# Expert up pass: two of three fetched token blocks summed on VectorE instead of one

## The reference

```python
idx = i1 * PEER_KEYS + i2                  # 8 heads x 16 picks = 128 expert rows for a token
g = jax.nn.softmax(cv, axis=-1)
u = expert_down[idx]
act = jax.nn.gelu(jnp.einsum('thkd,td->thk', u, xb).astype(jnp.float32), approximate=False)
v = expert_up[idx]
return jnp.einsum('thk,thkd->td', (g * act).astype(xb.dtype), v)
```

## Time and profile before

| | us |
|---|---|
| median of 3 runs | 4072.21 (4071.66 to 4079.16) |
| profiled execution | 4068.46 |
| its span, first to last instruction | 4066.7 |
| TensorE busy | 3796.6 (93%) |
| VectorE busy | 2708.6 (67%) |
| GpSimd busy | 1820.8 (45%) |
| ScalarE busy | 1664.8 (41%) |

### The profile page before, as it was taken

The page is one execution under the profiler, slowest core; times in us unless marked ns, Lnnn a source line. Parts: engine busy times, 40 slices in busy tenths (PEclk is TensorE's granted clock), DMA queues, the critical chain, the costliest instruction groups (busy, mean ns, idle before and its releaser), DMA issues. The chain is left out here.

```text
span 4066.7 us, 57361 instructions
## 1 busy us (share of the span) xinstructions
PE 3796.6 (93%) x21102; PEld 3193.4 (79%) x21102; DVE 2708.6 (67%) x4934; ACT 1664.8 (41%) x3225; POOL 1820.8 (45%) x1291
## 2 busy tenths in 40 slices
PE   6999899989899969998999999999969999999998
PEld 3877688866677869998999999999956777777776
DVE  3587411148775426688999999997756666666666
ACT  2111233358422431136777777777612222222222
POOL 3333233359544112133333333335546767676774
PEclk8999899999999989999999999999989999999999
DMA  4244333348666332276888888889999999999998
GB/s 158 69 150 150 120 97 124 103 160 263 183 196 190 103 123 73 62 259 231 269 274 274 266 281 268 271 272 352 364 309 349 352 347 350 336 336 349 347 349 290
DMA packets 641664, 957.80 MB, mean 236 GB/s; under 512 B 198900, under 2 KB 418820, under 8 KB 640516
## 3 DMA queue, kind: packets, MB, share of 16 engines
q1 hardware_dynamic: 311984, 407.35, 30.5%
q0 software_dynamic: 110592, 402.70, 28.3%
q10 hardware_dynamic: 218836, 144.47, 11.3%
HBM read 807.46 MB, written 146.93 MB: 235 GB/s over the span
## 5 line engine op out<-in xcount | busy, mean ns | idle before, releaser
L2034 POOL DMA_INDIRECT down_rows<-in_peer_down_dram,row_ids x384 | 464.3, 1209 | 830.3 <-DVE row_u L2174 743.4
L2055 PE MATMUL p_u<-h2T_hi,downT_hi 128*128 128x320 f32 x2048 | 657.2, 321 | 11.3 <-ACT gelu_out L2105 10.6
L2055 PE MATMUL p_u<-h2T_lo,downT_hi 128*128 128x320 f32 x2048 | 637.6, 311 | 0.0
L2055 PE MATMUL p_u<-h2T_hi,downT_lo 128*128 128x320 f32 x2048 | 637.3, 311 | 0.0
L2174 DVE CUSTOM_DVE_ANT_0 gate_rows<-down_rows,x_tok_rows 128x1024 f32<-128x1024 f32 x384 | 469.1, 1222 | 79.8 <-DMA down_rows<-in_peer_down_dram,row_ids 66.7
L2576 PE MATMUL p_y<-up_hi,coef_hi 128*128 128x512 f32 x1240 | 493.3, 398 | 18.6 <-DVE coef_lo L2468 9.2
L2576 PE MATMUL p_y<-up_lo,coef_hi 128*128 128x512 f32 x1240 | 485.9, 392 | 0.0
L2576 PE MATMUL p_y<-up_hi,coef_lo 128*128 128x512 f32 x1240 | 483.9, 390 | 0.0
L545 PE MATMUL p<-hT_hi,w_hi 128*128 128x512 f32 x1024 | 410.4, 401 | 7.1 <-POOL w_lo L499 7.1
L2055 PEld LDWEIGHTS p_u<-h2T_hi,downT_hi 128*128 128x128 f32 x2048 | 390.2, 191 | 13.7 <-issue 12.7
L545 PE MATMUL p<-hT_hi,w_lo 128*128 128x512 f32 x1024 | 399.9, 391 | 0.0
(11 more groups left out here) (337 smaller groups left out, 8081.1 us busy)
## 6 DMA issues: line engine op xcount, KB each, us to landing
down_raw<-in_peer_down_dram SPq DMA_DIRECT2D x128, 512.0 KB, 5.6
up_raw<-in_peer_up_dram SPq DMA_DIRECT2D x128, 512.0 KB, 5.7
scratch_gu<-gelu_out ACTq DMA_DIRECT2D x128, 320.0 KB, 5.1
gelu_in<-scratch_gu SPq DMA_DIRECT2D x128, 320.0 KB, 6.1
weights_in<-scratch_w SPq DMA_DIRECT2D x128, 320.0 KB, 6.9
w_raw<-in_w_in_dram SPq DMA_DIRECT2D x64, 512.0 KB, 4.2
scratch_w<-weights_out ACTq DMA_DIRECT2D x40, 512.0 KB, 8.1
scratch_w<-y_acc ACTq DMA_DIRECT2D x40, 512.0 KB, 7.0
```

Source lines behind the costliest of these rows:

```text
L2034: pool.indirect_dma_start(out=rows[:, c % RING, :], out_offset=None, in_=inp["peer_down"][0], in_offset=bass.IndirectOffsetOnAxis(ap=row_i ...
L2055: mm = pe.matmul(ps_u[half][:, 0:HD], d[:, n % 3, k, :], h2[h][:, k, half * HD:(half + 1) * HD], start=(j == 0), stop=(j == 3 * KD - 1))
```

## The change

Two of the three fetched blocks are now summed on VectorE (`NP = 1`, `NO = 2`): own fetches and own sums run over blocks 1 and 2, two a tile step, with a ring of 4; block 0 alone goes through TensorE, one quad a group, at slot 1, with a ring of 4. The first spread is made before the first group and each further one a group ahead. On GpSimd the four row fetches of a group stand behind the first low part and its own fetches (in group 1 behind the third). The id copy for the own blocks takes two blocks at a time. At the end, blocks 1 and 2 are finished first.

```diff
-    NP = NA - 1
-    OWN = NA - 1
-    FINISH = (*range(NP - 1), OWN, *range(NA, TB - 2), NP - 1, TB - 2, TB - 1)
-    RING = 6
+    NP = NA - 2
+    NO = NA - NP
+    FINISH = (*range(NP - 1), *range(NP, NA), *range(NA, TB - 2), NP - 1, TB - 2, TB - 1)
+    RING = 4
     SPREADS = 2 * NP
-    RING_OWN = 2
+    RING_OWN = 4
...
                 def fetch_own(c):
 
+                    a, k = NP + c // P, c % P
...
-                                            in_offset=bass.IndirectOffsetOnAxis(ap=ids_t[:, OWN, c:c + 1], axis=0)
+                                            in_offset=bass.IndirectOffsetOnAxis(ap=ids_t[:, a, k:k + 1], axis=0)
...
                 cut(0, 0)
                 cut(0, 1)
-                for r in range(4):
+                for r in range(RING):
                     fetch(r)
                 fetch_own(0)
+                fetch_own(1)
                 cut(0, 2)
                 cut(0, 3)
-                for r in range(4, RING):
-                    fetch(r)
-                fetch_own(1)
+                fetch_own(2)
+                fetch_own(3)
                 for g in range(1, GROUPS):
-                    r, c = (g - 1) * 4 * NP + RING, (g - 1) * GT + RING_OWN
-                    cut(g, 0)
-                    fetch_own(c)
-                    for i in range(4):
-                        fetch(r + i)
-                    cut(g, 1)
-                    fetch_own(c + 1)
-                    cut(g, 2)
-                    fetch_own(c + 2)
-                    for i in range(4, 8):
-                        fetch(r + i)
-                    cut(g, 3)
-                    fetch_own(c + 3)
-                for r in range((GROUPS - 1) * 4 * NP + RING, 4 * QUADS * NP):
-                    fetch(r)
-                for c in range((GROUPS - 1) * GT + RING_OWN, P):
+                    c = (g - 1) * GT * NO + RING_OWN
+                    for j in range(GT):
+                        cut(g, j)
+                        for i in range(NO):
+                            fetch_own(c + j * NO + i)
+                        if j == (2 if g == 1 else 0):
+                            for i in range(4):
+                                fetch(4 * g + i)
+                for c in range((GROUPS - 1) * GT * NO + RING_OWN, P * NO):
                     fetch_own(c)
...
                 def add_own(c):
...
-                    dve.wait_ge(own_added, c)
-                    dve.scalar_tensor_tensor(acc[:, OWN, :], own_rows[:, c % RING_OWN, :], coef[:, OWN, c:c + 1],
-                                             acc[:, OWN, :], ALU.mult, ALU.add).then_inc(own_added, 1)
+                    dve.scalar_tensor_tensor(acc[:, a, :], own_rows[:, c % RING_OWN, :], coef[:, a, k:k + 1],
+                                             acc[:, a, :], ALU.mult, ALU.add).then_inc(own_added, 1)
...
+                for q in range(NP):
+                    spread_rows(q)
                 for g in range(GROUPS):
                     for j in range(GT):
                         coefs(g, j)
                         if g:
-                            add_own((g - 1) * GT + j)
+                            for i in range(NO):
+                                add_own(((g - 1) * GT + j) * NO + i)
...
-                    for q in range(NP):
-                        spread_rows(g * NP + q)
+                    if g + 1 < GROUPS:
+                        for q in range(NP):
+                            spread_rows((g + 1) * NP + q)
...
                 done = 0
-                for j in range(GT):
-                    add_own((GROUPS - 1) * GT + j)
+                for i in range(GT * NO):
+                    add_own((GROUPS - 1) * GT * NO + i)
...
                             if base == 0:
                                 pe.wait_ge(g_lo_done, j + 1)
                                 pe.wait_ge(up_lo_done, j + 1)
-                            elif j % 2:
-                                quad(j // 2)
+                            elif j == 1:
+                                quad(0)
```

More of the change, by code:

```diff
@@ L2414, in _ @@
                         act.wait_ge(rows_kept, t + 1)
-                    elif t == OWN:
-                        act.wait_ge(own_added, P)
+                    elif t < NA:
+                        act.wait_ge(own_added, P * (t - NP + 1))
                     else:
@@ L2452, in add_own @@
                     dve.wait_ge(own_loaded[c % RING_OWN], 16 * (c // RING_OWN + 1))
[L2453 to L2454 removed]
+                    a, k = NP + c // P, c % P
+                    if c:
+                        dve.wait_ge(own_added, c)
+                    if k == 0:
+                        dve.tensor_scalar(acc[:, a, :], own_rows[:, c % RING_OWN, :], coef[:, a, 0:1], None, ALU.mult
                                           ).then_inc(own_added, 1)
                         return
[L2457 to L2459 removed]
+                    dve.scalar_tensor_tensor(acc[:, a, :], own_rows[:, c % RING_OWN, :], coef[:, a, k:k + 1],
+                                             acc[:, a, :], ALU.mult, ALU.add).then_inc(own_added, 1)
                 def coefs(g, j):
```

4 lines of the change are left out of this document (1 added, 3 removed).

## The result

The changed kernel takes 4198.05 us (median of 4 runs, 4187.55 to 4202.84), the kernel before, run beside it, 4072.1 (4071.66 to 4079.16). The ratio is 1.03, with a 95% interval of 1.0281 to 1.032. The prediction was 4089 us with a range of 4034 to 4110: the sign was right, the size far off. The profiled execution took 4202.84 us (span 4201.0), 134.4 us more than the one of before.

What follows compares the result with a forecast made beforehand. TensorE bounds the kernel before; after the change a VectorE-GpSimd loop would. Steady part +17, start -5, end +5 make +17 us on the profiled 4068.46, 4085.5; that run lay 3.7 under the median, so 4089 us, range 4034 to 4110.

Steps and rivals of the forecast that it cites:

- a loop of VectorE and GpSimd: Steady groups: 25.7 us of work plus 6.8 of collisions, 32.4 us against 31.85, +17 us over 30 groups; chance 45%.
- 25.7 us a group: VectorE's own work in a group of four steps and one spread, without collisions; alone it would fit under TensorE's 29.59.
- product at 17.3, just ahead of the low part (17.4): Step 3 of a group: product goes first, low part runs 18.1 to 20.4, coefficient low part is delayed, 1.5 us lost.
- 1.2, 1.5 and 1.7 to 1.9: Microseconds lost a group to GpSimd's low parts: before step 2's product, in step 3, and in next group's step 0.
- the fourth, the own sum: Step 2: GpSimd's low part gets in between the pair's two own sums at 12.6, runs until 15.0; 2.4 us lost.
- The claim of stability: Group loop: moving GpSimd half a microsecond either way gives the same 32.3 to 32.4 us, trusted to about 0.5 us.
- 1.24: Microseconds after the end of a pair of own sums at which GpSimd's next low part asks, with two fetches a step.
- Late weights: Step 3's weights land at 17.2 against 17.3 wanted: no cost in the sum, but no cover behind it.
- loads late on top of the loop: Rival: step 3's weights land late and lengthen every group; at +1 us, +47 us, 4119 us; chance 12%.
- Start: Before group 1: GpSimd skips the first quad's wait, loads come earlier; gain of 5 us, at most 11, at least -4.
- End: After the last step: eight own sums instead of four, two rounds of fetching in a ring of four; +5 us.
- The bound by DMA: Rival: DMA full at 362 GB/s, 30.4 us a group (30.6 with idle), 4034 us; DMA or TensorE bound, chance 28%.

Runs made afterwards that it cites:

- low_on_dve: Changed kernel with the tiles' low parts moved from GpSimd to VectorE, right behind each coefficient low part: 4033.03 us, ratio 0.9912.
- memset_low: Changed kernel with each GpSimd low part replaced by three memsets of the same tile, reading nothing from SBUF: 4051.65 us.
- low_first: Changed kernel with GpSimd reordered: low part directly behind a pair of own sums, ahead of the fetches, row fetches two a step in two steps: 4065.37 us, ratio 0.9989.
- gap_wait: Changed kernel with a one-column GpSimd memset between fetch and low part, the low part waiting for its semaphore: 4137.48 us.
- wait_both: Changed kernel with the first own fetch of a step waiting for both own sums in place of one: 4203.0 us.
- no_weights: Changed kernel loading the expert weights of only the first two tiles and using them for all: 4163.0 us.
- short_low: Changed kernel with GpSimd's low part over 64 of 1024 columns, the others left zero: 4066.72 us.
- order_only: Kernel before, with only the changed kernel's order of row fetches in group 1 and of spreads: 4073.14 us, ratio 0.9995.
- low_between: Changed kernel with low parts on VectorE, between gelu product and coefficient low part, where VectorE waited for ScalarE: 3990.76 us, ratio 0.9797.

## Why the prediction was wrong

**Right.** TensorE stops being the bound, and a loop of VectorE and GpSimd sets the pace. low_on_dve and memset_low show that the collision of the low parts with two-input operations is the cause, low_first that the order on GpSimd decides its size. The work on VectorE was well priced: 25.7 us a group, and 25.7 + 9.2 (lines above, per group: products 4 x 1.05, own sums 8 x 0.24, spread 2.64, `coef_lo` 4 x 0.1) + 0.9 late weights is 35.8 of the 35.98. That one pair in four carries a low part inside it was right too.

**The step that failed: "product at 17.3, just ahead of the low part (17.4)".** The prediction let the one that asks first in the record go first. The earlier trace rows have it so for a low part that GpSimd had waited for (0.66 us idle). All four low parts of a group stand directly behind a fetch here, with their inputs ready, and there a lead of up to 0.62 us is no lead. Instead of going first, or of losing 1.2 to 1.9 us to a low part already under way, spread and products lose the whole low part, 2.6 to 2.7 us. Three such terms were priced 1.2, 1.5 and 1.7 to 1.9 and came out at 2.63, 2.71 and 2.65; the fourth, the own sum, was priced 2.4 and is 1.95. gap_wait shows it by taking the head start away: blocked time falls to about 4.4 us a group (4 x 0.345 of products, 4 x 0.72 of `coef_lo`, 8 x 0.02 of own sums).

**A second error, of timing, beside it.** For the terms of 1.2 and of 1.7 to 1.9 the prediction had the low part start ahead of VectorE's operation, by 1.2 and 0.5 us. In the group shown the product is recorded 0.36 us and the spread 0.39 us ahead of it, because the fetches before it were held under VectorE's operations: counted from the pair that ended at 3839.35, the product stands at 7.85 us, as predicted (7.8), the low part at 8.2 and not at 6.6. By the prediction's own rule VectorE would have gone first in all three.

**The claim of stability failed with it.** "Moving GpSimd by half a microsecond either way ... gives the same 32.3 to 32.4" was said of a model in which the order of asking decides. The low part comes 2.10 us after a pair (3831.88 against 3829.78), not 1.24, because a fetch asked under the second sum is held. wait_both moved two of the low parts to 2.5 us and the time stayed, so half a microsecond does leave the sum as it is, but at 36 us and not at 32.3 to 32.4. No run puts the low part at 1.24 us, so what the timing alone is worth stays open; what the winner is worth gap_wait shows: 1.7 us a group with late weights that have grown from 0.8 to 3.6.

**Late weights: priced at nothing, with 0.1 us of cover.** In the changed kernel they add 0.9 us of waits a group; no_weights is 1.2 us a group shorter. Where the collisions shrink they take over: 3.6 us in gap_wait, 5.3 in short_low. The rival "loads late on top of the loop" was true in kind, and held back because the collisions were slower still. So 32.4 us was not reached in gap_wait either, where VectorE goes first: it takes 34.2.

**Start:** predicted -5, it was -2.0 in this profile and -1.8 in order_only. The prediction took only 5 of 11 us because of the transfers; the runs speak against that limit: with the same loads low_between takes 58.8 us there and memset_low 57.9, against 63.7. **End:** predicted +5, it was -2.6. Eight own sums stand there, but three follow at once (4155.99), and the fetch of the last lands in 5.32 us:

```profile
4155.99 1.20 DVE y_acc L2454
4157.19 0.26 issue
4157.45 1.93 POOL up_own_rows L2346
...
4162.81 5.32 DMA up_own_rows<-in_peer_up_dram,row_ids_turned
...
4169.36 0.68 DVE y_acc L2474
```

(Chain that ended last: start us, us, what.) From the last `coef_lo` (4151.60) to the first PSUM add of the last group are 17.8 us; in the kernel before that add stood behind the own sums that ended at 4035.5, 20.8 us after. There the last row fetches stood ahead of the own ones. I did not test the end alone.

**The bound by DMA** was wrong in its number: 362 GB/s was only what the kernel before asked for. low_between moves 376 GB/s at a share of 0.99, and in its group of 29.20 us TensorE never idles: 31.44 less the quad of 1.85 gives 29.59, and the group comes out 0.4 us under it. TensorE bounds it, with the DMA engines close behind. The Trainium skill, HBM Reference, section Specifications (TRN2), with about 425 GB/s for a core alone, spoke against my bound; no run here comes near that figure, but at 362 GB/s a group of 11.01 MB takes 30.4 us, and 29.2 could not have been had.

## What to carry to other kernels

Before moving work onto an engine that shares a path with another, mark each operation that can be held, and ask of the other engine's instruction not only when it starts but whether it stands queued and ready behind a running one. VectorE at 69 us in 100 had no room here, because each of GpSimd's four 2.4 us subtractions a group could stop it. The remedy was to move the 2.4 us operation off GpSimd into an idle gap of VectorE, where it takes 1.22 us: 3990.76 us, 2.0% under the kernel before and 4.9% under the changed one.

## What the runs showed of the hardware

- A two-input operation of VectorE and a GpSimd subtraction that reads SBUF exclude each other for their whole length; three memsets of the same tile (2.9 us) hold nothing. The Trainium skill, SBUF — State Buffer, section Who interferes with whom, says that VectorE's second input contends with a GpSimd instruction that reads SBUF and not with one that only writes it. By that rule the trace agrees.
- A low part of 1024 or 512 columns directly behind a fetch, its inputs ready, holds VectorE off from about 0.6 us ahead of its recorded start (117 of 117 at leads of up to 0.62 us), also across a small memset, and no longer once it waits for a semaphore (gap_wait). One of 64 columns does not (short_low). The Trainium skill, SBUF — State Buffer, section Who interferes with whom, says that the order of issue decides who is blocked; read with the recorded starts it gives the wrong winner here.
- An indirect DMA that GpSimd is asked for under a two-input operation of VectorE ends 0.80 to 0.85 us after it, and takes up to 2.0 us in place of 0.94; one that starts within 0.13 us of the operation's start can still run its usual 0.94 us. A fetch that runs first does not hold VectorE (own sums begun inside a fetch take 1.28 us). The Trainium skill, SBUF — State Buffer, section Who interferes with whom, infers that `tensor_tensor` does not hold descriptor generation back; the measurement differs.
